# Attention of the third layer: the four query tiles of each pair of heads taken in the order 128, 512, 256, 384 keys instead of 128, 256, 384, 512

## The reference

```python
s_s = jnp.einsum('bqgrd,bgqnkd->bgrqnk', qb, k_sel, preferred_element_type=f32)
s_s = s_s - slopes[None, :, :, None, None, None] * d_s[:, :, None].astype(f32)
m_s = (d_s >= 0)[:, :, None].reshape(bsz, G, 1, Q_BLOCK, n_sel * SEL_BLOCK)
p_s = _masked_softmax(s_s, m_s)
o_s = jnp.einsum('bgrqm,bgqmd->bqgrd', p_s, v_sel)
...
s_w = jnp.einsum('bqgrd,bkgd->bgrqk', qb, kwb, preferred_element_type=f32)
s_w = s_w - slopes[None, :, :, None, None] * d_w.astype(f32)
p_w = _masked_softmax(s_w, m_w)
o_w = jnp.einsum('bgrqk,bkgd->bqgrd', p_w, vwb)
return (gb[:, :, 0, :, :, None] * o_c + gb[:, :, 1, :, :, None] * o_s
        + gb[:, :, 2, :, :, None] * o_w)
```

## Time and profile before

| | |
|---|---|
| median of 3 runs | 1442.19 us (1440.94 to 1443.71) |
| the profiled execution, its own time | 1442.7 us |
| its span | 1439.8 us |
| PE busy in the span | 1312.5 us (91%) |
| DVE busy | 913.8 us (63%) |
| ACT busy | 407.9 us (28%) |
| POOL busy | 925.5 us (64%) |
| attention units, first scores to last values | 923.4 us to about 1099.6 us |

### The profile page before, as it was taken

The page is one execution under the profiler, slowest core; times in us unless marked ns, Lnnn a source line. Parts: engine busy times, 40 slices in busy tenths (PEclk is TensorE's granted clock), DMA queues, the critical chain, the costliest instruction groups (busy, mean ns, idle before and its releaser), DMA issues.

```text
span 1439.8 us, 22666 instructions
## 1 busy us (share of the span) xinstructions
PE 1312.5 (91%) x8136; PEld 1033.5 (72%) x8136; DVE 913.8 (63%) x1464; ACT 407.9 (28%) x782; POOL 925.5 (64%) x705
## 2 busy tenths in 40 slices
PE   5999879799998899999999899888888998999986
PEld 3777778578876688877777788555556876778874
DVE  6978796378999811299546507278784548852423
ACT  4165300414220123311210012467674200231111
POOL 6877301398999988999978737400002985578973
PEclk9999999899999999999999999899999999999998
DMA  4222100134323443344585212100003457623321
GB/s 166 81 81 73 44 3 2 30 125 108 95 81 95 161 154 100 92 123 132 140 281 165 73 45 68 50 1 2 2 1 119 152 147 217 187 94 96 100 77 71
DMA packets 86480, 137.94 MB, mean 96 GB/s; under 512 B 16512, under 2 KB 34432, under 8 KB 85376
## 3 DMA queue, kind: packets, MB, share of 16 engines
q1 hardware_dynamic: 48384, 88.10, 20.3%
q10 hardware_dynamic: 38016, 48.71, 10.7%
HBM read 119.02 MB, written 20.91 MB: 97 GB/s over the span
## 4 chain that ended last, share of the span: by engine, by line
PE 55%; DVE 21%; POOL 9%; issue 9%; ACTq 2%; ACT 2%; DMA 1%; POOLq 0%; DVEq 0%
PE ps L373 13%; PE ps L374 12%; PE ps L375 12%; POOL wh L1279 7%; PE ps L711 3%; DVE bigB L1812 3%; POOL wl L1281 3%; PE ps L723 3%; PE ps L700 2%; DVE ffL L1730 2%; ACTq L1046 2%; DVE bigB L1873 1%; PE ps L542 1%; DVE acc L1352 1%; DVE uL L1342 1%
## 5 line engine op out<-in xcount | busy, mean ns | idle before, releaser
L1279 POOL TENSOR_TENSOR wh<-raw,small 128x512 fp32r<-128x512 f32 x336 | 414.1, 1232 | 273.8 <-PE ps L375 264.1
L1281 POOL TENSOR_TENSOR wl<-raw,wh 128x512 fp32r<-128x512 f32 x336 | 498.5, 1484 | 26.4
L373 PE MATMUL ps<-uH,wh 128*128 128x512 f32 x672 | 268.0, 399 | 18.3 <-DVE uL L1342 13.6
L374 PE MATMUL ps<-uL,wh 128*128 128x512 f32 x672 | 263.4, 392 | 0.0
L375 PE MATMUL ps<-uH,wl 128*128 128x512 f32 x672 | 263.0, 391 | 0.0
L373 PEld LDWEIGHTS ps<-uH,wh 128*128 128x128 f32 x672 | 127.1, 189 | 50.0 <-POOL wl L1281 10.7
L374 PEld LDWEIGHTS ps<-uL,wh 128*128 128x128 f32 x672 | 127.3, 189 | 27.3 <-issue 1.7
L375 PEld LDWEIGHTS ps<-uH,wl 128*128 128x128 f32 x672 | 127.4, 190 | 26.7
L373 PE MATMUL ps<-ffH,wh 128*128 128x512 f32 x256 | 103.1, 403 | 16.1 <-POOL wl L1281 12.7
L374 PE MATMUL ps<-ffL,wh 128*128 128x512 f32 x256 | 99.9, 390 | 0.0
L375 PE MATMUL ps<-ffH,wl 128*128 128x512 f32 x256 | 99.9, 390 | 0.0
(11 more groups left out here) (381 smaller groups left out, 2500.1 us busy)
## 6 DMA issues: line engine op xcount, KB each, us to landing
raw<-wstream SPq DMA_DIRECT2D x336, 256.0 KB, 2.6
b_powers_scratch<-bigB ACTq DMA_DIRECT2D x4, 1024.0 KB, 5.0
c_powers_scratch<-bigB ACTq DMA_DIRECT2D x8, 512.0 KB, 4.1
lags_scratch<-lag_rows_scratch ACTq DMA_DIRECT2D x8, 512.0 KB, 9.4
bigB<-b_powers_scratch ACTq DMA_DIRECT2D x4, 1024.0 KB, 6.0
bigB<-lags_scratch ACTq DMA_DIRECT2D x4, 1024.0 KB, 6.9
bigB<-c_powers_scratch ACTq DMA_DIRECT2D x4, 1024.0 KB, 9.4
hT<-x ACTq DMA_DIRECT2D x4, 512.0 KB, 7.2
```

Of the source, the lines that this page charges most:

```text
L373: pe.matmul(out, lh, rh, start=first, stop=False)
L374: pe.matmul(out, lh, rl, start=False, stop=False)
L1279: pool.tensor_tensor(wh[:, j, :], raw[:, j, :], zero_ap.to_broadcast([128, 512]), ALU.add).then_inc(half_lead, 1)
L1281: pool.tensor_tensor(wl[:, j, :], raw[:, j, :], wh[:, j, :].bitcast(f32), ALU.subtract).then_inc(half_split, 1)
```

## The change

Only the list `UNITS` changes, and with it the order on PE, DVE and ACT; POOL and SP have the same instructions in the same order. The number and the sizes of all instructions stay as they were. The places 0 to 7 now have widths 128, 128, 512, 512, 256, 256, 384, 384.

```diff
-        UNITS = [(t, qt, b) for t in range(KT) for qt in range(TT) for b in range(2)]
+        UNITS = [(t, qt, b) for t in range(KT) for qt in (0, 3, 1, 2) for b in range(2)]
```

## The result

The changed kernel took 1459.92 us (median of 7 runs, 1454.26 to 1461.57) against 1443.71 us (median of 7, 1440.94 to 1449.46) of the kernel before. The ratio of the runs is 1.0096, with a 95% interval of 1.0072 to 1.0121: slower, as forecast, but by far more than the 0.3% forecast, and above the forecast range of 1444.4 to 1450.3 us.

What follows compares the result with a forecast made beforehand. PE was taken as nearest to full in the attention, idle where turns wait for DVE's weighing. Pairs +4.3, start +0.5, drain -1.1, clock +0.9 on 1442.7, less 0.5 for the median, gave 1446.8 us, range 1444.4 to 1450.3.

Steps and rivals of the forecast that it cites:

- The idle times: PE's waits before turns in each pair: 1.59 us at place 2, none at 4, 1.70 at 6; +4.3 over seven pairs.
- The prediction's own test: Formula checked on the kernel before: at place 6, 0.93 us plus 0.74 for POOL's tables gives 1.67, where 1.60 is printed.
- The drain: End of the attention: the last two units have 384 keys instead of 512, so the output product starts sooner, -1.1 us.
- POOL's tables: DVE's multiplications beside POOL's table writing at place 6: a narrower unit saves nothing, the loss stays 0.74 us.
- The start: Fill and first pair of the attention: third scores 512 columns instead of 256, +0.5 us, bounds 0 and 1.6.
- The clock: Half-clock stretches behind PE's long gaps: about one more at 1.8 us, taken as 0.9 us, bounds 0 and 3.
- Rival 2: The clock falls behind most long gaps in the pairs: three to seven falls more, 1450 to 1457 us, chance 0.07.
- five times not: Rival 2's counterargument: of six such gaps in the kernel before, the clock fell behind one and not behind five.

Runs made afterwards that it cites:

- a_fill: The changed kernel with eight dummy transposes on PE ahead of the turns of place 2 and of place 6 in every pair; 1444.10 us.
- b_fill: The kernel before with dummy transposes on PE in every pair, two ahead of the turn of place 2 and eight ahead of place 6; 1441.84 us.
- b_longpool: The kernel before with a third, 256-wide POOL instruction ahead of the two tables; 1452.28 us against 1444.08.

## Why the prediction was wrong, by its own steps

- **The idle times: right.** Places 2 and 6 came out within 0.01 us, place 4 has none, and the two pairs at full clock are within 0.05 us of the forecast. The turns waited 24.3 us in all for L1887, where about 25 were forecast. The seven pairs cost 4.5 us (a_fill against b_fill) where 4.3 were summed. The prediction's own test was weaker than it says: at place 6 with POOL's tables the 0.74 came from the pair times and not from the formula.
- **The drain: right.** From the turn of the last place 6 to the output product 1119.30 - 1112.26 = 7.04 us, before 1102.15 - 1094.03 = 8.12: -1.1, as summed.
- **POOL's tables: right in size.** The two multiplications of 384 keys took 1.16 us beside POOL and take 0.75 without it: 0.41 more, as much as 512 keys lose. So the loss is not in proportion to the unit's own length, and the 0.74 stays (21.91 - 21.16 = 0.75 between pairs with and without tables). The Trainium skill, SBUF — State Buffer, section "SBUF: two separate sides", says that the engines' shared port pair is an exclusive lock, held for the whole instruction. The trace agrees in so far that the narrower unit saved nothing. The equal loss alone does not show a lock: the multiplications lie beside POOL's tables for the same 0.62 to 0.63 us in both kernels (from 965.17 to 964.43 + 1.36, and from 1067.13 to 1066.40 + 1.36), and a slowdown by a fixed factor over that time would give the same 0.41. For a full stop over that time 0.41 is also too little, unless an instruction gets some of its work done before it has to wait. The small product ahead of them (L1885) speaks for the lock. Beside POOL's tables it takes 0.49 us instead of 0.16 and ends at 1067.10, about where the first table does (half of 1.36 us behind 1066.40 is 1067.08, an estimate); in b_longpool, where POOL's first instruction is shorter, it takes 0.27 us and ends with that one, at 987.89. The sum needed only the 0.74.
- **The start: came out lower, and by the clock.** +0.5 was summed; from the first scores to the first turn of place 6 the trace shows 943.86 - 924.0 = 19.9 us against 21.9, 2.0 less. The slow stretch in the fill ended earlier (clock 0.80 in the window 928 to 936, 0.51 in the kernel before). What the start costs at equal clock no run shows: a_fill and b_fill differ there by 1.0 us the same way, and again in the clock.
- **The clock: the step that failed.** I read one fall behind six gaps of 1.60 us as a rate, gave it to the added gaps, priced a fall at the 1.56 us of the earlier trace rows, and took 0.9 us with 3 as bound. The seven pairs of the profiled execution took 168.40 us against 148.75. With the pairs at full clock as measured (21.90 and 21.17 us, before 21.24 and 20.50) they would have taken 151.8 and 147.2: of the 19.65 us 4.6 are the chain and 15.0 are falls, 16.6 in the changed kernel less 1.6 in the one before. So the term of 0.9 measured 15.0, and 4.6 + 15.0 - 2.0 - 1.1 make the 16.5 us of the attention. Both factors, the number of falls and the price of one, were too small. A fall cost 3.0 us, because five of the six lasted 6.8 us instead of 3.4. And falls came behind four of the gaps of place 6, which the prediction had left at their old price because they are no longer than before (1.70 against 1.67).
- **Why the old gap became harmful: probably the narrower work around it.** From the turn of place 5 to that of place 6 PE had 0.80 + 0.81 + 0.42 = 2.03 us of work before, and has 0.58 + 0.59 + 0.42 = 1.59 now, by the prediction's own pieces, beside an equal gap. This fits three runs: two dummy transposes at this gap take back what eight do; work at place 2 does not; 0.2 us more idle time in the ascending order brings the falls there. It is argued and not shown. The dummies change both the gap and the work ahead of it, the longer POOL work changes the gap alone, and no run widens or narrows the work at an unchanged gap; whether the work ahead of the gap or that behind it counts is open too. What is shown is that idle time before the turn of place 6 is needed for most of the falls.
- **Rival 2 named the right case**, with a chance of 0.07, but its price of 1450 to 1457 us is too low as well. It asked for three to seven falls more than before, and the trace has five more in the attention; at 1.56 us each they would be 7.8 us, and they took 15.0. Its argument against itself, "five times not", took the gap's length for all that matters.

## What to carry to other kernels

When a reordering moves narrow work next to an existing idle time of the matmul engine, price the clock for that gap anew, even if the gap itself does not grow, and read how much work stands on both sides of it. One fall in a trace is no rate; it can mean that the kernel runs close to an edge, and the range must then reach over what a fall in every repetition costs. The distance of two pairs in this software pipeline (engines that work on different units at the same time) was computed to within 0.1 us from a chain and its cover, for the changed and the descending order and for the deeper ascending one; the effect of more POOL work on the gap was not (0.22 us for 0.4). More depth was the best answer to the idle time here (1421.87 us), and with it the order is worth the opposite.

## What the runs showed that was not expected

- Useless work made a kernel faster: eight and eight dummy transposes in each pair took the changed kernel from 1459.92 to 1444.10 us, and two in each pair did the same (1444.64).
- The kernel before is itself close to the edge. Its own runs lie between 1439.8 and 1451.4 us, and a POOL instruction of 0.48 us in six pairs cost 8.2 us.
- Starting POOL's tables two units later made the kernel before faster by 8.3 us (1435.77 against 1444.08), of which the chain explains 6 x 0.74 = 4.4; the rest fits fewer falls. In the two profiled executions that is one fall of 1.6 us less; how many there are in the others no trace shows.
